# A two-block transformer kernel on one core: other start addresses in SBUF for the split weights and the packed inputs

## What is computed

```python
for l in range(2):                       # first block, 272 tokens
    h = h + 0.5 * swiglu(rmsnorm(h), w_gate, w_up, w_down)   # 1024 -> 2816 -> 1024
    proj = rmsnorm(h) @ w_in                                 # 1024 -> 3584
    h = h + concat(retention(proj), differential_attention(proj)) @ w_out
    h = h + 0.5 * swiglu(rmsnorm(h), ...)
h = rmsnorm(h)[16:]
for i in range(2):                       # second block, 256 tokens
    h = h + 0.5 * swiglu(rmsnorm(h), w_in, w_out)
    h = h + (short_convolution(rmsnorm(h)) if i == 0 else dilated_attention(rmsnorm(h)))
    h = h + 0.5 * swiglu(rmsnorm(h), w_in, w_out)
```

## Time and profile before

| | us |
|---|---|
| median of 3 runs | 2171.89 |
| lowest, highest | 2171.26, 2173.23 |
| the profiled execution, its own time | 2173.17 |
| its span in the trace | 2171.1 |
| TensorE busy | 2158.2 (99%) |
| VectorE busy | 1558.4 (72%) |
| ScalarE busy | 1220.8 (56%) |
| GpSimd busy | 458.1 (21%) |

### The profile page before, as it was taken

How to read it: one execution, slowest core, us unless ns; L and a number is a source line. 1 busy time by engine, 2 the same in 40 slices (tenths; PEclk the granted TensorE clock), 3 DMA queues, 4 the chain that set the end, 5 groups by cost and what they waited for, 6 DMA issues and landing times.

```text
span 2171.1 us, 38708 instructions
## 1 busy us (share of the span) xinstructions
PE 2158.2 (99%) x15614; PEld 2039.8 (94%) x15614; DVE 1558.4 (72%) x2588; ACT 1220.8 (56%) x2017; POOL 458.1 (21%) x499
## 2 busy tenths in 40 slices
PE   9999999999999999999999999999999999999999
PEld 9999999999999999988988999889888999999888
DVE  8655977665665586876697586975876688887863
ACT  6444466444544456665566444655655576676652
POOL 1000522420350052231053000430331011101420
PEclk9999999999999999999999999999999999999999
DMA  8655435975786543565466554755555576674653
GB/s 279 206 165 174 152 118 147 240 191 166 197 208 183 174 156 117 172 198 194 155 213 204 186 185 147 230 193 192 181 190 177 168 198 173 175 230 141 225 178 106
DMA packets 424082, 395.35 MB, mean 182 GB/s; under 512 B 16816, under 2 KB 420400, under 8 KB 423905
## 3 DMA queue, kind: packets, MB, share of 16 engines
q1 hardware_dynamic: 410336, 375.22, 55.1%
q0 software_dynamic: 13280, 17.33, 3.8%
q10 hardware_dynamic: 288, 0.34, 0.0%
HBM read 389.20 MB, written 7.41 MB: 183 GB/s over the span
## 4 chain that ended last, share of the span: by engine, by line
PE 93%; DVE 3%; ACT 2%; DMA 1%; issue 1%; SPq 0%; ACTq 0%
PE ps L1687 29%; PE ps L1683 25%; PE ps L1685 16%; PE ps L1686 16%; DMA t<-attn_w_qkv 1%; DVE t L1178 1%; PE ps L2027 1%; PE ps L2026 1%; PE ps L2025 1%; PE ps L1702 1%; PE ps L1803 0%; PE ps L1848 0%; PE ps L1977 0%; DVE t L1213 0%; PE ps L1993 0%
## 5 line engine op out<-in xcount | busy, mean ns | idle before, releaser
L1687 PE MATMUL ps<-t 128*128 128x256 f32 (+1 forms) x5456 | 1548.2, 284 | 0.0
L1687 PEld LDWEIGHTS ps<-t 128*128 128x128 f32 x5456 | 1029.2, 189 | 0.1
L1178 DVE TENSOR_TENSOR t<-t 128x1024 fp32r<-128x1024 f32 (+1 forms) x722 | 876.4, 1231 | 174.5 <-ACT t L836 174.0
L1685 PE MATMUL ps<-t 128*128 128x272 f32 (+1 forms) x3036 | 876.2, 289 | 0.2 <-DVE t L1405 0.2
L836 ACT ACTIVATE t<-t 128x1024 fp32r<-128x1024 f32 (+1 forms) x722 | 729.9, 1030 | 256.7 <-PE ps L1687 229.1
L1686 PE MATMUL ps<-t 128*128 128x272 f32 (+1 forms) x3036 | 866.0, 285 | 0.0
L1683 PE MATMUL ps<-t 128*128 128x512 f32 x2420 | 840.2, 390 | 0.0
L1685 PEld LDWEIGHTS ps<-t 128*128 128x128 f32 x3036 | 571.5, 188 | 5.9 <-issue 3.4
L1686 PEld LDWEIGHTS ps<-t 128*128 128x128 f32 x3036 | 574.4, 189 | 0.9
L1683 PEld LDWEIGHTS ps<-t 128*128 128x128 f32 x2420 | 454.1, 188 | 95.0
L760 POOL TENSOR_TENSOR t<-t 128x256 f32<-128x256 f32 x110 | 100.6, 914 | 694.2 <-ACT t L954 694.2
(11 more groups left out here) (200 smaller groups left out, 1560.1 us busy)
## 6 DMA issues: line engine op xcount, KB each, us to landing
t<-ffn_w_in SPq DMA_DIRECT2D x88, 1024.0 KB, 5.3
t<-ffn_w_gate SPq DMA_DIRECT2D x42, 1024.0 KB, 5.5
t<-ffn_w_up SPq DMA_DIRECT2D x42, 1024.0 KB, 7.4
t<-attn_w_qkv SPq DMA_DIRECT2D x72, 512.0 KB, 4.8
t<-ffn_w_down SPq DMA_DIRECT2D x32, 1024.0 KB, 5.2
t<-ffn_w_out SPq DMA_DIRECT2D x32, 1024.0 KB, 5.3
t<-w_in SPq DMA_DIRECT2D x28, 1024.0 KB, 5.0
t<-ffn_w_down SPq DMA_DIRECT2D x16, 768.0 KB, 4.4
```

What stands on the lines that cost most here:

```text
L1178: dve.tensor_tensor(wlo[:, plan.place[n], 0:nk, :], kept(u)[:, 0:nk, half * P:half * P + P], f32(whi[:, plan.place[n], 0:nk, :]), ALU.subt ...
L1685: pe.matmul(o, hi, xhi, start=i == 0, stop=False)
L1687: ins = pe.matmul(o, lo, xhi, start=False, stop=i == r.nk - 1)
```

## The change

Two tensors that nothing reads or writes are allocated around the split weights: 64 bytes ahead of `whi`, 192 bytes behind `wlo`. `whi` and `wlo` move by 64 bytes, to 192 mod 256 (and 192 mod 1024); everything allocated behind them moves by 256 bytes and keeps its place mod 256. The packed view of `x` then begins 136 elements (544 bytes) behind `x`, that of `a` 200 elements (800 bytes) behind `a`: both at 416 mod 1024. `c_yy` and `d_y` go with the rest from 416 to 672 mod 1024, `y_close` from 672 to 928. No instruction is added, removed or moved, and no semaphore.

```diff
--- before.py
+++ after.py
@@ -452,8 +452,10 @@
 
     with ctx:
         raw = alloc(ctx, [P, NRAW, 8, PAIR])
+        ahead = alloc(ctx, [P, 16])
         whi = alloc(ctx, [P, NP, 8, P], F32R)
         wlo = alloc(ctx, [P, NP, 8, P], F32R)
+        behind_weights = alloc(ctx, [P, 48])
         h = alloc(ctx, [P, KC, T])
         x = alloc(ctx, [P, KC, 2, T], F32R)
         acc = alloc(ctx, [P, T])
@@ -554,7 +556,7 @@
             whole = t[:, :, :, :].rearrange("p k m c -> p (k m c)")
             return whole[:, first:first + n * 2 * SEQ].rearrange("p (k m c) -> p k m c", k=n, m=2)
 
-        x_close, a_close, y_close = close(x, KC, HALF_LINE), close(a, FCH, HALF_LINE), close(y, KC, 0)
+        x_close, a_close, y_close = close(x, KC, 136), close(a, FCH, 200), close(y, KC, 0)
 
         raw_first = raw[:, 0:3, :, :].rearrange("p r k n -> p (r k n)").rearrange(
             "p (k u c) -> p k u c", k=KC, u=2)
```

## The result

The changed kernel takes 2189.2 us (median of 4 runs, 2188.7 to 2189.56) against 2172.1 for the kernel before beside it: a ratio of 1.0081, 95% interval 1.0069 to 1.0093. It is 17 us slower, outside the range of the prediction, 2160 to 2185.

The account below looks back on a forecast made before the run. TensorE's matmul stream was taken to bound the kernel; three terms of 0 against a median of 2171.89, with a 0.9 us lean to a small gain, made 2171.0 us. The 8-in-10 range was 2160 to 2185.

Parts of the forecast that it names:

- What bounds the kernel: TensorE's matmul stream, busy 99% at 2.4 GHz; the edit matters only through the distance between matmul starts, some 171 us overhead.
- Part one: Packed input at 416 instead of 672 mod 1024: taken as 0, with 0 and -2.7 us as its ends.
- The lean of 0.9 us: A third of the reach of the packed input's move, taken as a small gain: 2171.9 - 0.9 = 2171.0.
- Part two: Weights at 192 instead of 128 mod 256: taken as 0, bounded by -14.5 and +20.3 us.
- the slower rival: Packed 256-token stages lose their 32-byte relation of input to weights: half of the bound, +10.2 us, 2182.1; chance 0.24.
- Against: nothing shows that 32 from the weights, rather than 32 from a multiple of 64, is the cause.: The prediction's argument against packed stages slowing when input minus weights goes from 32 to 224 bytes mod 256.
- The comparison of the earlier trace: 256 columns: 116.7 ns in the convolution's packed view, 119.2 in the second mixer's 272-column layout; address or chunk distance matters.
- The rival of no effect: Start addresses at steps of 64 bytes do not matter anywhere: 2171.9 us; measurably the same as the forecast, which had 0.46.
- The faster rival: 272-column stages gain part of what separates them from packed ones: half of the bound, -7.2 us, 2164.7; chance 0.30.
- the wheel of four relations: In 272-token stages, inputs pass through 0, 64, 128, 192 mod 256; moving weights 64 bytes only turns this one notch.
- Part three: Other engines: VectorE's reads and writes shift 64 bytes apart; taken as 0, with 3 us possible in either direction.

Follow-up runs that it names:

- part one alone: Against the kernel before, only the packed view of `x` moved, to 416 mod 1024 in place of 672; weights stayed at 128 mod 256: 2171.36 us, ratio 1.0000.
- the best kernel: Against the kernel before, 272-column chunks of `x` and of the gated products 1280 bytes apart, 160 bytes past the weights mod 256: 2159.44 us, ratio 0.9951.

## Why the prediction was wrong

**What bounds the kernel.** Right: the loss is in the distance between starts, with the same clock and the same waits.

**Part one, 0 to -2.7 us.** Right at zero. The lean of 0.9 us had nothing behind it: part one alone gave a ratio of 1.0000. Dilated attention's 1.4 ns is not the address mod 1024, since its inputs take 351.6 for three at 416 as at 672.

**Part two, 0 taken between -14.5 and +20.3 us.** This is the step that failed. The measured +17 lies inside the bound, but the value was taken from the wrong rows: the 272-column stages, "whose mean did not depend on the sequence". Those stages mix four relations, so their mean says nothing about a stage that has one. The mean does depend, too: after the change it was 376.1, 379.5 and 374.4 ns a triple in three stages, and only their sum is near zero, by luck. It was known that the packed stages have one relation and would get another, and that nothing excluded 32 from being what makes them fast. What the runs showed in place of the 0 is the slower rival: +15.8 us on pairs and +4.1 on packed triples, and the experiments tie them to the relation. The sizes inside the rival were off in both directions: a packed triple lost 3 to 5 ns (the rival's bound was 3 x 2.6 = 7.8) and a pair 6.5 (5.2). That their sum, 19.9 us, comes near the bound of 20.3 is luck. Pairs take 2420 x 346.7 ns = 839 us, two fifths of the time, and carry most of the loss.

**"Against: nothing shows that 32 from the weights, rather than 32 from a multiple of 64, is the cause."** Shown now: 96 and 224 are as far from a multiple of 64, and cost 10 and 5 ns a packed triple, while 16 costs none. The comparison of the earlier trace rows, left open between the place and the distance of the chunks, is settled too. With chunks 1280 bytes apart the 256 columns that the second mixer reads out of 272 stand at one relation, and a triple of them takes 358.7 ns at 96 and 355.1 at 224, where packed ones take 359.9 and 355.1. The relation accounts for it.

**The rival of no effect** had both addresses cost the same. With the same instructions, moving inputs against weights by 64 bytes cost 0.7 to 0.9%. The Trainium skill, "SBUF — State Buffer", section "SBUF: two separate sides", has TensorE's port wait for no one. To conclude from it that the start address is free is wrong here, by these ratios; whether a port is where the time goes, no run here shows.

**The faster rival** priced the way to the best kernel and misplaced it. The change gave the 272-column stages next to nothing, because it turned the wheel of four relations without stopping it, and what single stages won and lost cancelled. Stopping it at 160 bytes brought them to 370.3, 123.4 a matmul where the bound had 123.3; 13.8 us in the bound, 11.1 measured.

**Part three** was right: nothing of VectorE shows.

Open is what in TensorE or its memory makes the relation count, why the shapes rank it differently, and what chooses between two rhythms of one relation. No run here settles it.

## What to carry over

Where a stream of matmuls sets the time, treat the start of the moving operand minus the start of the weights, mod 256 bytes, as a parameter of each shape, and lay chunks at a distance that keeps it constant; then measure several values, one per stage in a single run, and a good one in more than one stage, since a relation can have two rates. Don't carry a good value from one width to another. And a mean over mixed cases is no evidence for a stage that has only one of them.

## What the runs showed of the hardware

The relation of moving to stationary operand, mod 256 bytes, moves a pair of 512 and 256 float32r columns between 346.7 and 353.3 ns, three of 256 between 350.0 and 359.9, three of 272 between 370.0 and 379.7, at a granted clock of 1.00 (2.4 GHz). The best values are 832, 840 and 888 cycles: over their 768, 768 and 816 columns 64, 72 and 72 cycles are left. Two elements may count: pairs on `x` 8 bytes past the weights took 353.3, measured in one stage, and at 0 and 16 bytes 346.7. The same relation can run at two rates in two stages of one execution (346.7 and 353.3 at 224 bytes). In the changed kernel the slow rate is an alternation: 240 and 229 ns in turn from a 512-column matmul to its partner, against 228.3 before.
